# Constant full-width products among the narrow products of a router

## The chip, the cores and the metric

## What is computed

Two blocks, one after the other, on a sequence of 256 tokens of width 1024, all in fp32. The first block has two layers with attention and a grouped mixture of experts; the second has four layers with retention or attention and a plain MLP. The change concerns the mixture of experts of the first block. Cut to what matters:

```python
h = modulate(rmsnorm(x, ffn_norm_g[layer]), sh2, sc2)        # h * (1 + sc2) + sh2
x = x + g2[:, None, :] * grouped_moe(h, router_w, router_bias, w_gate, w_up, w_down)

def grouped_moe(h, router_w, router_bias, w_gate, w_up, w_down):
    scores = jax.nn.sigmoid(hf @ router_w)                    # 256 tokens x 16 experts
    # the best of 4 groups for each token, the best 2 experts in it, their shares
    for e in range(N_EXPERTS):
        a = jax.nn.silu(hf @ w_gate[e]) * (hf @ w_up[e])
        y = y + combine[:, e:e + 1] * (a @ w_down[e])
```

sh2, sc2 and g2 are rows of a product of silu(c) with a weight matrix; they are the same for all tokens.

## The kernel before

The tokens are two blocks of 128. Weights stream from HBM in pieces; ScalarE and VectorE split each into a high and a low part in fp32r, and TensorE does three fp32r products for one. Small products whose result decides the routing are in full fp32; each of them shows in the trace as two matmul instructions.

Each engine has one queue of instructions in program order. On TensorE the order is written out by hand; for each of the two mixture-of-experts layers (plan.moe0, plan.moe1), right behind the attention before it, it is:

1. `shift_product` (L1106, records on L1112): the router's weights times the shift row, eight products of 16 columns.
2. `modulations` (L1143, records on L1133): the sum over partitions of two rows of modulation, which give the scale. Eight products of one column. Together these are called the scale rows' products here.
3. `turn_x` (records on L1252): x, which the attention's output has just been added to, is transposed in sixteen blocks of 128x128 into the four banks of the PSUM tensor Y.
4. `route_product` (L1115, records on L1124): sixteen products of 16 columns, two token blocks for each of eight blocks k of the model's width. It waits for the router's weights (VectorE, L2616), and with every second k for the copy of one bank of Y (VectorE L2622 for banks 0 and 1, ScalarE L2004 for 2 and 3).
5. `keep_busy(8)` (L1231, records on L1234): eight constant products, the unit matrix times a triangle of ones, written to the first 128 columns of Y, where nobody reads them.
6. `place_tokens` (L1404 to L1408): counts of tokens for each group. It waits for VectorE, which has taken the router's sums (L2627) and made the sigmoid's and the groups' comparisons in some thirteen small steps, up to L2547.
7. `keep_busy(10)`, then the gathering of tokens and the experts' loop, for whose gate, up and down products the weights stream in.

`wait_free(pe, use)` waits until the pair of PSUM banks that `use` names has been emptied by its last reader. There are two pairs; the router's sums and the shift's stand in one and the scale rows' sums in the other.

Of the kernel before, what the change touches and what calls it, by code (L numbers as in the profile page):

```python
# [14 lines left out]
P = 128  # L15
# [362 lines left out]
def build(nc, w, table, out, rel_scratch):  # L378
# [3 lines left out]
    with ctx:  # L382
# [62 lines left out]
        ident, upto_m = squares[:, 0:P], squares[:, P:2 * P]  # L445
# [220 lines left out]
        def pair(use):  # L666
            return pairs[use.u % 2]
# [29 lines left out]
        def wait_free(eng, use):  # L697

            if use.u >= 2:
                eng.wait_ge(emptied[use.u % 2], use.u // 2)  # L700
# [280 lines left out]
        def _(pe):  # L981
# [134 lines left out]
            def route_product(m):  # L1116

                blocks = [k for bank in range(4) for k in (bank, bank + 4)]
                pe.wait_ge(router_ready, m.nth + 1)
                for i, k in enumerate(blocks):  # L1120
                    if i % 2 == 0:
                        pe.wait_ge(x_lower_copied if k < 2 else x_upper_copied, 2 * m.nth + k % 2 + 1)
                    for b in range(TB):
                        last = nc.tensor.matmul(pair(m.router)[:, b * EXPERTS:(b + 1) * EXPERTS],  # L1124
                                                turned_x[:, norm_at[k] + b * P:norm_at[k] + (b + 1) * P], router_g[:, k, :],
                                                start=(i == 0 and b == 0), stop=(i == KD - 1 and b == TB - 1))
                last.then_inc(fill_done, 1)

            def mod_product(m, out):

                wait_mod(pe, m, 8)
                for f in range(4):
                    last = nc.tensor.matmul(out[:, f:f + 1], mod_total(m)[:, f * P:(f + 1) * P], ones_col,  # L1133
                                            start=True, stop=True)
                return last
# [6 lines left out]

            def modulations(ms, use):  # L1143
                wait_free(pe, use)
                for i, m in enumerate(ms):
                    last = mod_product(m, pair(use)[:, 4 * i:4 * i + 4])
                last.then_inc(fill_done, 1)
# [83 lines left out]
            def keep_busy(n):  # L1231

                for _ in range(n):
                    nc.tensor.matmul(Y[:, 0:P], ident, upto_m, start=True, stop=True)  # L1234
# [217 lines left out]
            def experts(m):  # L1452
                turn_x(m.norm)
                route_product(m)
                keep_busy(8)
                place_tokens(m)
# [211 lines left out]
            use = plan.columns  # L1668
# [12 lines left out]
            for j in range(6):  # L1681
                token_product(plan.a_proj[j])

                use, ones_m = plan.cum[j], ones_col.to_broadcast([P, P])
                if j == 0:
# [5 lines left out]
                                     start=False, stop=True).then_inc(fill_done, 1)  # L1691
# [11 lines left out]
                if j >= 2:  # L1703
                    mod_product(STAGES["a"][j - 2], first_mods[j - 2]).then_inc(a_modulated, 1)
            attention(plan.att_a, HD, q_area, k_area, v_area, qT_area, kT_area, o_area, HD,
                      attention_done(plan.att_a), values_kept(plan.a_proj[5]), MOD[0] + G1)
            shift_product(plan.moe0)
            modulations(*plan.out_a_mods)
            experts(plan.moe0)
            for mod_use in plan.kv_mods:  # L1710
# [54 lines left out]
            use = plan.ckvT  # L1765
# [41 lines left out]
            def queries_turned(j):  # L1807
# [3 lines left out]
                      attention_done(plan.att_b), values_kept(plan.kv_up[-1]), MOD[1] + G1, queries_turned)  # L1811
            shift_product(plan.moe1)
            modulations(*plan.out_b_mods)
            experts(plan.moe1)

# [1326 lines left out]
```

## Time and profile before

| | |
|---|---|
| median of 3 runs | 2551.22 us (2542.8 to 2553.99) |
| profiled execution | 2548.41 us |
| its span, first to last instruction | 2546.6 us |
| TensorE, records of matmuls | 2426.7 us busy, 95% |
| VectorE | 1694.0 us, 67% |
| ScalarE | 1304.5 us, 51% |
| chain that ended last | TensorE 83%, VectorE 10%, ScalarE 3% |
| mean granted clock of TensorE | 0.987 |

The span is that of one execution under the profiler. "Busy" counts the time in which an engine has at least one record; a matmul's record holds its latency too, so records overlap and a busy TensorE is not one at its peak. For the time that one of a row of equal products takes, the distance between their starts, or the time in the chain, divided by their number, is to be used, not the length of a record. The chain that ended last is followed back from the last instruction, at each step to what released it.

### The profile page before, as it was taken

What the parts mean: (1) busy time and instruction counts of PE and PEld (TensorE: products, weight loads), DVE (VectorE), ACT (ScalarE), POOL (GpSimd) and SP (SyncE); (2) the same over time, 40 slices, a digit from 0 to 9 for tenths busy, and PEclk for the clock granted to TensorE, in tenths of its full rate; (3) what the DMA queues carried; (4) which work ended last, traced back from release to release, by engine and by line L of the source; (5) the groups of instructions that cost most, each with busy time, mean ns of one, the idle gap of its engine ahead of it and who ended that gap; (6) DMA issues with size and microseconds to landing.
All of it is one profiled execution on the core that took longest, in us unless ns stands there. A gap on an engine that the chain in (4) does not pass through costs nothing.

```text
span 2546.6 us, 31351 instructions
## 1 busy us (share of the span) xinstructions
PE 2426.7 (95%) x12650; PEld 2057.4 (81%) x12650; DVE 1694.0 (67%) x1521; ACT 1304.5 (51%) x1795; POOL 93.4 (4%) x121
## 2 busy tenths in 40 slices
PE   4989999999899999999999999899997999999999
PEld 3878888887788888879878888788886888987887
DVE  5767988887769787857455565565557655645654
ACT  2555777434547666634445445454455544444443
POOL 1000000111000000000000001000010000000000
PEclk8999999999999999999999999999999999999999
DMA  8815999984519897945535775155551555553553
GB/s 303 289 34 185 368 368 356 358 308 168 217 39 327 301 331 276 365 160 174 195 128 176 190 273 182 61 175 194 193 180 52 184 195 190 174 198 132 177 188 116
DMA packets 229568, 539.80 MB, mean 212 GB/s; under 512 B 20880, under 2 KB 27568, under 8 KB 229424
## 3 DMA queue, kind: packets, MB, share of 16 engines
q1 hardware_dynamic: 207264, 471.82, 53.1%
q0 software_dynamic: 15520, 59.77, 6.4%
q10 hardware_dynamic: 6640, 6.20, 1.3%
q8 instruction: 100, 1.64, 0.3%
q14 instruction: 44, 0.36, 0.0%
HBM read 533.54 MB, written 4.19 MB: 211 GB/s over the span
## 4 chain that ended last, share of the span: by engine, by line
PE 83%; DVE 10%; ACT 3%; issue 2%; DMA 1%; POOL 1%; ACTq 0%; DVEq 0%
PE pair L1041 7%; PE Y L1206 6%; PE Y L1204 6%; PE Y L1215 6%; PE pair L1469 5%; PE pair L1470 5%; PE pair L1475 5%; PE pair L1084 4%; PE pair L1077 4%; PE pair L1078 4%; PE pair L1050 4%; PE Y L1514 3%; PE Y L1516 3%; PE Y L1524 3%; PE pair L1010 2%; PE pair L1019 2%
## 5 line engine op out<-in xcount | busy, mean ns | idle before, releaser
L2316 DVE TENSOR_TENSOR w_low<-raw,w_high 128x2048 fp32r<-128x2048 f32 (+2 forms) x450 | 1016.0, 2273 | 438.8 <-ACT w_high L1858 437.4
L1858 ACT ACTIVATE w_high<-raw 128x1024 fp32r<-128x1024 f32 (+1 forms) x900 | 896.4, 1049 | 554.1 <-PE pair L1470 169.3
L1077 PE MATMUL pair<-w_high,hT 128*128 128x512 f32 (+1 forms) x596 | 233.1, 392 | 1.6 <-ACT work L1913 0.8
L1078 PE MATMUL pair<-w_high,hT 128*128 128x512 f32 (+1 forms) x596 | 231.9, 390 | 0.0
L1206 PE MATMUL Y<-w_high,gated_low 128*128 128x512 f32 x528 | 205.9, 390 | 0.0
L1204 PE MATMUL Y<-w_high,gated_high 128*128 128x512 f32 x528 | 205.9, 390 | 0.0
L1041 PE MATMUL pair<-hT,w_high 128*128 128x512 f32 x768 | 183.0, 390 | 0.5 <-DVE work L2762 0.5
L1041 PEld LDWEIGHTS pair<-hT,w_high 128*128 128x128 f32 x768 | 142.6, 188 | 29.7 <-DVE work L2762 0.9
L1469 PE MATMUL pair<-w_high,rounded 128*128 128x512 f32 x384 | 154.8, 403 | 0.8 <-DVE gated_low L2660 0.8
L1470 PE MATMUL pair<-w_high,rounded 128*128 128x512 f32 x384 | 152.2, 396 | 0.0
L1084 PE MATMUL pair<-w_low,hT 128*128 128x512 f32 (+1 forms) x596 | 146.8, 388 | 4.0 <-DVE w_low L2316 4.0
L1084 PEld LDWEIGHTS pair<-w_low,hT 128*128 128x128 f32 x596 | 110.7, 188 | 28.8 <-DVE w_low L2316 6.5
L1077 PEld LDWEIGHTS pair<-w_high,hT 128*128 128x128 f32 x596 | 113.0, 190 | 25.6 <-issue 1.6
L1078 PEld LDWEIGHTS pair<-w_high,hT 128*128 128x128 f32 x596 | 113.0, 190 | 22.5
L1215 PE MATMUL Y<-w_low,gated_high 128*128 128x512 f32 x528 | 130.4, 389 | 0.0
L1514 PE MATMUL Y<-w_high,gated_high 128*128 128x512 f32 x320 | 125.1, 391 | 3.8 <-DVE gated_low L2660 3.8
L1010 PE MATMUL pair<-hT,w_high 128*128 128x256 f32 x512 | 125.2, 285 | 0.5
L1516 PE MATMUL Y<-w_high,gated_low 128*128 128x512 f32 x320 | 124.8, 390 | 0.0
L1012 PE MATMUL pair<-hT,w_high 128*128 128x256 f32 x512 | 124.5, 283 | 0.0
L1215 PEld LDWEIGHTS Y<-w_low,gated_high 128*128 128x128 f32 x528 | 99.1, 188 | 20.6
L1206 PEld LDWEIGHTS Y<-w_high,gated_low 128*128 128x128 f32 x528 | 99.3, 188 | 19.8
L1204 PEld LDWEIGHTS Y<-w_high,gated_high 128*128 128x128 f32 x528 | 99.3, 188 | 19.8
(395 smaller groups left out, 3984.3 us busy)
## 6 DMA issues: line engine op xcount, KB each, us to landing
raw<-in_exp_w_gate SPq DMA_DIRECT2D x128, 512.0 KB, 4.6
raw<-in_exp_w_up SPq DMA_DIRECT2D x128, 512.0 KB, 4.8
raw<-in_exp_w_down SPq DMA_DIRECT2D x128, 512.0 KB, 4.6
raw<-in_w_up SPq DMA_DIRECT2D x128, 512.0 KB, 4.6
raw<-in_w_down SPq DMA_DIRECT2D x128, 512.0 KB, 4.3
raw<-in_ret_w_in SPq DMA_DIRECT2D x96, 512.0 KB, 4.7
work<-in_w_mod POOLq DMA_DIRECT2D x40, 1024.0 KB, 8.1
raw<-in_ret_w_out SPq DMA_DIRECT2D x32, 512.0 KB, 4.0
```

Of the source, the lines that this page charges most:

```text
L1041: last = nc.tensor.matmul(ps[:, f, :], high[:, k, fs], hT[:, :, kk, :], start=(kk == 0), stop=False)
L1077: nc.tensor.matmul(ps[:, b, 0:n], in_high[:, k0 + kk, bs], high[:, k, :], start=(kk == 0), stop=False)
L1078: last = nc.tensor.matmul(ps[:, b, 0:n], in_low[:, k0 + kk, bs], high[:, k, :], start=False, stop=False)
L1084: last = nc.tensor.matmul(ps[:, b, 0:n], in_high[:, k0 + kk, b * P:(b + 1) * P], low[:, k, :], start=False, stop=(kk == k_blocks - 1))
L1204: nc.tensor.matmul(y, high_in[:, kk, b * P:(b + 1) * P], high[:, k, ns], start=(first and kk == 0), stop=False)
L1206: last = nc.tensor.matmul(y, low_in[:, kk, b * P:(b + 1) * P], high[:, k, ns], start=False, stop=False)
L1215: last = nc.tensor.matmul(y, high_in[:, kk, b * P:(b + 1) * P], low[:, k, ns], start=False, stop=False)
L1469: nc.tensor.matmul(out(m, v), x_high, high[:, k, :], start=(h == 0 and k == 0), stop=False)
L1470: last = nc.tensor.matmul(out(m, v), x_low, high[:, k, :], start=False, stop=False)
L1514: nc.tensor.matmul(y, gated_high[:, v % 2, 2 * h + k, 0:WIN], high[:, k, ns], start=(first and k == 0), stop=False)
L1858: nc.scalar.activation(w_high[:, s % HIGH, part], raw[:, s % RAW, part], ACT.Copy).then_inc(high_ready, 1)
L2316: V.tensor_tensor(w_low[:, s % RAW, 0:n], part, w_high[:, s % HIGH, 0:n].bitcast(F32), ALU.subtract).then_inc(low_ready, 1)
```

## The change

Two places on TensorE get constant products of the same kind as `keep_busy` has: the unit matrix times the triangle of ones, 128 columns each, in full fp32. Three stand ahead of the scale rows' products, behind the wait for their pair of banks, and are written to the second bank of that pair. Two stand in the router's product behind its third block k and two behind its sixth, written to Y as in `keep_busy`. What is computed stays as it was.

```diff
@@ route_product
                         last = nc.tensor.matmul(pair(m.router)[:, b * EXPERTS:(b + 1) * EXPERTS],
                                                 turned_x[:, norm_at[k] + b * P:norm_at[k] + (b + 1) * P], router_g[:, k, :],
                                                 start=(i == 0 and b == 0), stop=(i == KD - 1 and b == TB - 1))
+                    if i in (2, 5):
+                        keep_busy(2)
                 last.then_inc(fill_done, 1)
@@ modulations
                 wait_free(pe, use)
+                for _ in range(3):
+                    nc.tensor.matmul(pair(use)[:, 512:512 + P], ident, upto_m, start=True, stop=True)
                 for i, m in enumerate(ms):
                     last = mod_product(m, pair(use)[:, 4 * i:4 * i + 4])
                 last.then_inc(fill_done, 1)
```

## Rows read from the trace of the kernel before

**Rows 1.** The page: span, and its part 1.

```profile
span 2546.6 us, 31351 instructions
PE 2426.7 (95%) x12650; PEld 2057.4 (81%) x12650; DVE 1694.0 (67%) x1521; ACT 1304.5 (51%) x1795; POOL 93.4 (4%) x121
```

**Rows 2.** Chain that ended last, layer 0: start us, us, what, how many.

```profile
201.75 1.69 PE pair L1112 x16
203.44 1.82 PE pair L1133 x16
205.27 3.41 PE Y L1252 x16
208.68 3.63 PE pair L1124 x32
212.31 3.36 PE Y L1234 x16
...
215.78 0.36 PE pair L1404 x2
```

**Rows 3.** The same chain in layer 1.

```profile
750.88 1.69 PE pair L1112 x16
...
754.34 3.18 PE Y L1252 x16
757.52 3.77 PE pair L1124 x32
```

**Rows 4.** Table of stretches: its us, TensorE busy (instructions), granted clock, DMA share, GB/s.

```profile
201.60:205.00 3.40, 3.40 (x33) 1.00 0.00 0
205.05:208.40 3.35, 3.35 (x18) 0.50 0.30 98
208.50:211.80 3.30, 3.30 (x33) 1.00 0.00 0
211.90:215.20 3.30, 3.30 (x17) 0.50 0.00 0
...
754.60:758.00 3.40, 3.40 (x19) 0.50 0.24 81
758.05:761.40 3.35, 3.35 (x31) 1.00 0.00 0
```

**Rows 5.** Timeline of TensorE, transposes elsewhere: start us, us, line, shape, idle before.

```profile
1526.23 0.60 PE L1252 MATMUL Y<-squares,x 128*128 128x128 f32 x4
1527.77 1.53 PE L1252 MATMUL Y<-squares,x 128*128 128x128 f32 x12 [0.94 <-DVE x L2436]
```

**Rows 6.** Timeline, weight loads of the ten constant products behind the counts, layer 0.

```profile
216.86 2.31 PEld L1234 LDWEIGHTS Y<-squares 128*128 128x128 f32 x20
```

**Rows 7.** Timeline of TensorE, runs of narrow products elsewhere.

```profile
487.78 2.73 PE L1133 MATMUL pair<-squares,work 128*128 128x1 f32 x24
525.63 1.84 PE L1133 MATMUL pair<-squares,work 128*128 128x1 f32 x16
232.51 2.29 PE L1447 MATMUL pair<-logs,rounded 128*128 128x4 f32 x20
781.50 2.29 PE L1447 MATMUL pair<-logs,rounded 128*128 128x4 f32 x20
```

**Rows 8.** Table of stretches behind those four runs, in the order of their times.

```profile
235.80:239.10 3.30, 3.30 (x10) 0.50 1.04 377
491.90:495.10 3.20, 3.20 (x9) 0.50 0.98 384
528.00:531.50 3.50, 3.50 (x17) 1.00 1.03 397
783.70:787.10 3.40, 3.40 (x16) 1.00 1.07 390
```

**Rows 9.** Timeline of VectorE in layer 0: first copy of the transposes, last step before counting.

```profile
206.76 1.29 DVE L2622 COPY work<-Y 128x512 f32<-128x512 f32 x2 [0.67 <-PE Y L1252]
...
215.47 0.17 DVE L2547 TENSOR_TENSOR route<-route 128x8 f32<-128x8 f32 x1
```

## Prediction

> **What bounds the kernel now.** I read the head of the page first: the span is 2546.6 us and TensorE has records in 95% of it [rows 1]. One number for the whole says little of two short stages, so I then read the chain of waits in the stretch where the change sits, once for each mixture-of-experts layer. In layer 0 the chain runs on TensorE alone from 201.75 to 215.67 us: the shift's sixteen narrow products, the scale rows' sixteen, the sixteen transposes of x, the router's thirty-two, then the sixteen instructions of the existing filler, and at 215.78 the counting products of the routing [rows 2]. (A product in full fp32 is two instructions, so eight shift products are sixteen rows.) The stretch from the first shift product to the end of the router's product is what the change touches. It lasts 208.68 + 3.63 - 201.75 = 10.56 us in layer 0 and 757.52 + 3.77 - 750.88 = 10.41 us in layer 1 [rows 2, 3]. Nothing idles in it: TensorE waits for nobody, so what is put there lengthens it unless it gives time back.
>
> What it could give back is the clock. The table of stretches has the granted clock beside the busy time [rows 4]. In layer 0 the engine is busy all of 201.6 to 205.0 at full clock (2.4 GHz) with narrow products, then the clock stands at 0.50 (1.2 GHz) from 205.05 to 208.40, over the transposes; it is full again while the router's product runs, and 0.50 again from 211.90 to 215.20, over the filler. Layer 1 repeats this: 0.50 from 754.60 to 758.00, full after that. So both layers show the same order: narrow products, a fall, transposes at half clock, narrow products at full clock, a second fall. I take it that a run of narrow products makes the clock fall, and that wide work brings it back. The change mixes wide work into both runs.
>
> **What the first fall costs.** The sixteen transposes take 3.41 us in layer 0 [rows 2]. At full clock four take 0.60 us and twelve 1.53 [rows 5], so one more costs (1.53 - 0.60) / 8 = 0.116 us and sixteen 1.86. The first fall costs 3.41 - 1.86 = 1.55 us a layer, and this is on the path.
>
> **What the second fall costs.** It begins at about 211.9, and the router's product ends at 212.31 [rows 2, 4]. Of the router's time only the last 0.4 us are at half clock, at most 0.2 us lost. The filler that follows takes 3.36 us slow, but its time is not on a path of its own: when the router's product ends, VectorE takes the logits and works a chain of small steps until 215.47 + 0.17 = 215.64, when the first counting product may go [rows 9]. That product comes at 215.78 [rows 2]. So a fast filler gives back at most 0.1 us; past that, VectorE is late. The price of the second fall in the kernel before is 0.2 to 0.3 us.
>
> **The change, part by part.** (a) Three full-width constant products ahead of the scale rows' products are six instructions. The twenty instructions of the same product at full clock take 2.31 us [rows 6], 0.1155 each; so 0.69 us, at half clock 16 in 3.36 us [rows 2], 0.21 each and 1.26. (b) Two products at each of two places in the router's product are eight instructions: 0.92 us fast, 1.68 slow. Both parts are on the path, since nothing idles there. They bring no wait of their own: the pair of banks has been waited for by the same function already, and the bank of Y that (b) writes has been read by then, since the router's first block waits for that copy.
> (c) The order of other engines hardly moves. With (a) VectorE gets the scale sum 0.69 us later, and so builds the router's weights later. In layer 0 it sat 0.67 us for the transposes before its first copy of them at 206.76 [rows 9]. If the transposes run fast, the copy becomes the later one: it can start about a microsecond after the scale products, takes half of 1.29 us, and the router's product could start some 1.7 us after them, against 1.86 of transposes. I take 0 for this wait and keep 0.3 as a bound.
> (d) The stage with nothing slow: shift 1.69, (a) 0.69, scale 1.82 (its last few at half clock), transposes 1.86, router 32 instructions at 0.11 us, 3.50 (sixteen shift instructions of the same form take 1.69 [rows 2], 0.106 each; 3.63 with its slow tail), and (b) 0.92. Sum 10.48 us. Against 10.56 and 10.41 that is -0.08 and +0.07, together 0.0.
> So even if the clock never falls, the filler costs what it saves: 1.61 us a layer in, 1.55 and the slow tail out. If the first fall stays in a layer, its 1.55 us come on top: +1.47 in layer 0, +1.62 in layer 1, taken as +1.5. If the second fall also comes before the longer router's product is done: in layer 0, with both falls where they were, 10.1 us have passed at 211.86 with 3.4 of them at half rate, so 8.4 us of the 10.48 are done; of the other 2.08, 1.7 are done in 3.4 slow microseconds and 0.38 fast. That is 13.9 us, +3.3 a layer, the upper bound.
>
> **Will the clock stay up?** The nearest rows are other runs of narrow products. After sixteen scale-type instructions (1.84 us) between wide products at 525.63 the clock stayed full; three such runs in the experts' loops are alike, and the first stands for them [rows 7, 8]. After twenty-four (2.73 us, 487.78) it fell to 0.50 for 491.90 to 495.10 [rows 7, 8]. After twenty router-like instructions (2.29 us) it fell in layer 0 (at 235.80) and after the same twenty in layer 1, at 781.50, it stayed full [rows 7, 8]; the outcome differs between two passes of the same code. After thirty-two in a row it fell in all three runs that rows 2 to 4 hold. The change makes 16 + 16 with 0.69 us of wide work between, and 12 + 12 + 8 with 0.46 us twice. Each run by itself is like those that kept the clock, but the wide work between two of them is short: 0.69 us, where the runs that kept it stood alone among long wide stretches. I put an even chance on the first fall in each layer, and somewhat under even on a second fall that bites.
>
> A rule of notes on the chip speaks to this. The Trainium skill, "TensorE: Matmul & The Clock Gate", section "What's actually happening", puts the half clock down to an idle engine. The trace disagrees: the fall at 205 follows 3.40 us busy of 3.40 [rows 4]. By that rule filler could change no clock here and the sum would be the cost alone, the third case below.
>
> **The rivals.**
> 1. Forecast: the first fall is avoided in one layer and stays in the other: 0.0 + 1.5 = +1.5 us. For it: the two layers meet their falls at different points of the same code (before the transposes of 205.27 in one, after those of 754.34 have begun in the other [rows 2 to 4]), so they need not fare alike.
> 2. The change does all that it says: no fall in either layer, 0.0 us. For it: the runs of sixteen. Against: 0.69 us of wide work among 4.2.
> 3. It does not do what it says, and the kernel is slower: the first fall stays in both layers, +3.0 us. The place is the shift and scale stage; the price is the filler's own 1.61 us a layer on a path without idle time; it decides as soon as one layer keeps its fall. With second falls that land in the longer router's product it goes to +6.6. Past 0.5% it would take 12.8 us, twice this bound.
> 4. The transposes do not keep the clock up by themselves, so that one fall lasts through the router's product: transposes 3.41, router 32 x 0.213 = 6.8, (b) 1.68, with 4.2 ahead 16.1 us a layer, +11 in all, 2562. Rows 4 speak against it: in layer 0 the clock was back at 208.50 behind transposes alone. The Trainium skill, same page, section "Part 4: PE-mode transpose", says that a transpose does not count as TensorE being busy; this trace disagrees, and without this sentence the case rests on rows as before.
>
> **How the numbers follow.** Case 1 has 0.42, case 2 0.20, case 3 0.35 (of it 0.15 for more than +4), case 4 0.01, and 0.02 for things not seen. The profiled execution took 2548.4 us, span 2546.6 and 1.8 around it; with +1.5 it would be 2549.9. The median of the runs is 2551.2, 2.8 above, so I predict 2551.2 + 1.5 = 2552.7. The cases alone give 2551.2 to 2557.8. The runs of before reach from 2542.8 to 2554.0, 8 us below and 3 above their median, so a median of a few runs can be off by some 5 us either way: the range is 2546 to 2559. A measurement tells about 0.5% (12.8 us) from no change. No case but the fourth comes near it, so the chance of "same" is 0.95; faster 0.02 for the runs' own spread, slower 0.03 for that and case 4.
>
> **What would show it.** In each layer of the changed kernel: six and eight more instructions of the constant product, 0.1155 us each; transposes in 1.9 us with granted clock 1.00 where the fall is gone, 3.4 where not; the stage from the first shift product to the end of the router's product at 10.4 us, or 12.0, or up to 13.9; about 3.4 us from that end to the first counting product, whatever the clock, with TensorE idle before it if the filler ran fast. The prediction is wrong if that last interval shrinks with the clock, if the clock stays low over the router's product, or if stages away from the routing differ by more than a few microseconds.

## The result and the profile after

| | before | changed |
|---|---|---|
| median, executions of the first comparison | 2549.91 us (2542.8 to 2554.1, 7) | 2564.17 us (2554.07 to 2567.37, 7) |
| ratio, 95% interval | | 1.0038 [1.002, 1.0057] |
| profiled execution | 2548.41 us | 2566.04 us |
| its span | 2546.6 us | 2564.2 us |
| mean granted clock in it | 0.987 | 0.984 |

The forecast was 2552.7 us in a range to 2559; the time is 5 us past its upper end. Two later comparisons of the same two kernels came out smaller: 2556.06 against 2553.94, ratio 0.9998 [0.9983, 1.0014], and 2557.94 against 2555.15, ratio 1.0014 [1.000, 1.0027]. The ratios are those on record for the sets of executions; the medians of the first comparison alone would give 1.0056. So the size of the loss is itself a question, and is taken up below.

The page of the changed kernel, its first lines, against [rows 1]:

```profile
span 2564.2 us, 31405 instructions
PE 2445.1 (95%) x12678; PEld 2074.4 (81%) x12678; DVE 1693.8 (66%) x1521; ACT 1304.6 (51%) x1795; POOL 93.9 (4%) x121
```

Twenty-eight more matmul instructions, as counted, and the other engines as busy as before. The span is 17.6 us longer, TensorE 18.4 us busier. Twenty-eight instructions of 0.1155 us are 3.2.

The chain that ended last, in layer 0 of the changed kernel (start us, us, what), answers to [rows 2]. L1148 are the three added products, L1135 the scale rows' (L1133 before), L1256 the transposes, L1238 the filler:

```profile
206.71 1.69 PE pair L1112 x16
208.40 0.76 PE pair L1148 x6
209.16 2.37 PE pair L1135 x16
211.53 3.52 PE Y L1256 x16
215.04 2.37 PE pair L1124 x12
217.41 1.04 PE Y L1238 x4
218.46 2.37 PE pair L1124 x12
220.83 1.04 PE Y L1238 x4
221.87 1.52 PE pair L1124 x8
```

The reader is to compare the router's instructions: 12 in 2.37 us, 0.20 each, where 32 took 3.63 before, 0.11 each. The stage, from 206.71 to 221.87 + 1.52, lasts 16.7 us; before it lasted 10.56. The table of stretches says why (us, TensorE busy, granted clock, DMA share, GB/s), against [rows 4]:

```profile
206.70:209.90 3.20, 3.20 (x32) 1.00 0.00 0
210.10:213.40 3.30, 3.30 (x17) 0.50 0.31 99
213.50:216.80 3.30, 3.30 (x18) 0.50 0.00 0
216.90:220.20 3.30, 3.30 (x17) 0.50 0.00 0
220.30:223.60 3.30, 3.30 (x17) 0.50 0.00 0
223.70:227.00 3.30, 3.30 (x17) 0.50 0.00 0
227.20:230.50 3.30, 3.30 (x29) 1.00 0.02 5
```

The clock falls once, at 210.0, in the middle of the scale rows' products, and is back only at 227.0, behind the filler that follows the router. In the kernel before it fell at 205.0, by 0.1 to 0.2 us ahead of the transposes (205.27 in the chain), and was back behind them. Layer 1 of the changed kernel, timeline of TensorE, against [rows 3]:

```profile
762.58 1.85 PE L1112 MATMUL pair<-router_w,mod 128*128 128x16 f32 x16
...
767.11 3.65 PE L1256 MATMUL Y<-squares,x 128*128 128x128 f32 x16
...
778.95 3.76 PE L1238 MATMUL Y<-squares 128*128 128x128 f32 x16
```

From 762.58 to 778.95 are 16.4 us, against 10.4. The two stages account for 6.1 + 6.0 = 12.1 of the 17.6 us. But the first shift instruction of layer 0 comes at 206.71 and not at 201.75, so 5.0 us are lost before anything changed has run. The rows for the attention ahead of it, before and then changed:

```profile
160.00:180.00 20.00, 15.27 (x122) 1.00 0.19 63
```

```profile
160.00:180.00 20.00, 15.66 (x99) 0.74 0.17 56
```

Here too the clock is down for half of the stretch in one execution and not in the other, in code that is the same. Slow stretches come and go from execution to execution, in many places of the kernel: in the first two profiles of the kernel before, one of 23.9 us at 34 us is there once and not the other time, one of 10.2 us at 165 us the other way round.

### The profile page after: what moved, and what is told of

It is laid out like the page before. It is cut to its first block, busy times and chain, and to the rows that moved or that the text cites. A ratio compares the mean times of both kernels' runs of the same rounds, so it can differ in the third digit from the quotient of the medians.

```text
span 2564.2 us, 31405 instructions
## 1 busy us (share of the span) xinstructions
PE 2445.1 (95%) x12678; PEld 2074.4 (81%) x12678; DVE 1693.8 (66%) x1521; ACT 1304.6 (51%) x1795; POOL 93.9 (4%) x121
## 4 chain that ended last, share of the span: by engine, by line
PE 82%; DVE 10%; ACT 4%; issue 2%; DMA 1%; POOL 1%; ACTq 0%; DVEq 0%; POOLq 0%
PE pair L1041 7%; PE Y L1210 6%; PE Y L1208 6%; PE Y L1219 6%; PE pair L1473 5%; PE pair L1474 5%; PE pair L1479 5%; PE pair L1084 4%; PE pair L1077 4%; PE pair L1078 4%; PE pair L1050 4%; PE Y L1518 3%; PE Y L1520 3%; PE Y L1528 3%; PE pair L1010 2%; PE pair L1019 2%
```

## Experiments

**One part at a time, and more of it.** Four kernels on one chip: the changed one again, two that leave out one hunk of the change each, and one with more of the first hunk and none of the second. The last is, against the changed kernel,

```diff
-                for _ in range(3):
+                for _ in range(8):
                     nc.tensor.matmul(pair(use)[:, 512:512 + P], ident, upto_m, start=True, stop=True)
...
-                    if i in (2, 5):
-                        keep_busy(2)
```

> The changed kernel once more, unaltered, for a second profile of its two router stages (first shift product to the end of the router's product; 16.7 and 16.3 us in the first profile, 10.56 and 10.41 before). Theory A (the half-clock stretch that starts behind the shift and scale products lasts through transposes and router's product whenever it begins before the transposes do, and the filler in the router's product is too thin at half clock to end it): each stage is either near 10.5, near 12, or at 16 to 17 us, depending on where the fall lands; the kernel 3 to 14 us slower than before. Rival B (the added products cost their own 1.6 us a layer and the rest of the first result is the luck of other stages): stages of 10.5 to 13.9 us, time +2 to +6 us.

> Only the three constant products ahead of the scale rows' products. Theory A: 0.7 us more work a layer, a fall that can still begin in the scale products; then the slow stretch may last through the router's product, without the 0.92 us (1.7 slow) of filler there: stages near 9.6, 11.2 or 15 to 16 us; time 0 to +8 us. Rival B: +1.4 us in all. Rival C (the harm is the filler in the router's product, which is absent here): stages of at most 11.3 us, time within 2 us of before.

> Only the two times two constant products in the router's product. Theory A: the first fall stays where it was in the kernel before, at the start of the transposes, and these end it: stages of 11.4 to 12.3 us where it lands so, up to 17 where it lands elsewhere; time +2 to +8 us. Rival B: +1.8 us in all. Rival C: both stages at 15 us or more, with the clock at half through the router's product.

> Eight constant products (sixteen instructions, 1.85 us) ahead of the scale rows' products and none in the router's product. Theory A: the run of narrow products is now split by a wide stretch longer than either run, so the first fall is gone in both layers: transposes in 1.9 us at full clock, stages at 1.7 + 1.85 + 1.7 + 1.86 + 3.5 = 10.6 us in every execution, time -2 to +1 us against before. Rival B: +1.85 us a layer on top of what was there, stages of 12.3 us, +3.7 us in all.

A second profile of the kernel before was taken later:

> The kernel before, unaltered, for a second profile of its two stages. Theory A: 8.8 to 15 us each, one of the values of the copies (0,0) in the sixty stages plus at most 0.3. Rival B: 10.4 to 10.6 again.

And the changed kernel and the eight products were compared once more:

> The changed kernel unaltered, for more executions: its two comparisons so far gave 1.0038 [1.002, 1.0057] and 0.9998 [0.9983, 1.0014]. Theory A: an execution's time is set by how many slow stretches it meets; the ratio comes out between the two, 1.000 to 1.003, with a spread of runs of 15 us or more. Rival D (the first comparison is the true size): 1.003 or more.

> Eight constant products ahead of the scale rows' products, none in the router's product, once more; the first comparison gave 0.9984 [0.9973, 0.9996]. Theory A: the first fall is gone in both layers again (transposes in 1.8 us), a fall may still begin in or behind the router's product; ratio 0.997 to 0.9995. Rival B: 1.001.

What they gave. The stage is read from the timeline, from the first shift instruction to the first instruction behind the router's; "fall" is the first step to 0.50 behind the first shift instruction, with how long the clock stayed there.

| kernel | ratio to before | layer 0: fall at, for; stage | layer 1 |
|---|---|---|---|
| before, first profile | | +3.4, 3.4 us; 10.56 | +3.9, 3.4 us; 10.42 |
| before, second profile | | +3.0, 20.5 us; 14.06 | +2.8, 20.5 us; 14.23 |
| changed, first profile | 1.0038 [1.002, 1.0057] | +3.4, 17.1 us; 16.68 | +3.8, 17.1 us; 16.37 |
| changed, second comparison | 0.9998 [0.9983, 1.0014] | +3.4, 17.1 us; 16.67 | +9.5, 13.7 us; 11.34 |
| changed, third comparison | 1.0014 [1.000, 1.0027] | +3.5, 17.1 us; 16.65 | +9.6, 10.2 us; 11.19 |
| three ahead of scale alone | 1.0013 [0.9993, 1.0033] | +3.8, 13.7 us; 14.67 | +9.6, 3.4 us; 9.54 |
| two times two in the router alone | 1.0016 [1.0003, 1.0029] | +3.2, 3.4 us; 12.48 | +3.1, 3.4 us; 12.55 |
| eight ahead of scale | 0.9984 [0.9973, 0.9996] | +10.7, 3.4 us; 10.66 | +9.6, 13.7 us; 11.64 |
| the same again | 0.9985 [0.9973, 0.9997] | +10.7, 3.4 us; 10.67 | +10.3, 10.2 us; 11.03 |

The row that matters most is the second. The kernel before, untouched, has the long slow stretch too. Its chain in layer 0:

```profile
206.39 1.69 PE pair L1112 x16
208.08 2.21 PE pair L1133 x16
210.29 3.52 PE Y L1252 x16
213.80 6.64 PE pair L1124 x32
220.44 3.60 PE Y L1234 x16
224.04 0.43 PE pair L1404 x2
```

Transposes in 3.52 and a router's product in 6.64 us, against 3.41 and 3.63 in [rows 2]. The 10.56 and 10.42 us that the prediction started from are not the kernel's stage but two draws of it. Rival B expected 10.4 to 10.6 again here and falls; it falls with the changed kernel's 16.7 too, which it put at no more than 13.9. Rival C, that the filler in the router's product does the harm, expected both stages with the filler in the router's product alone at 15 us or more; they were 12.5, with full clock over the first 3.0 to 3.1 of the router's 5.6 us. It expected at most 11.3 us without that filler; three ahead of scale alone has 14.67. So neither part is needed for the long stretch. Theory A comes nearest so far: 14.67 stands near its "15 to 16", 9.54 near its "9.6", 12.5 near its "11.4 to 12.3". But it missed twice. It had the clock stay down whenever the fall comes before the transposes start, and with two times two in the router alone the falls at 3.2 and 3.1 us came 0.5 and 0.7 us before they started and lasted 3.4 us only. And it had the changed kernel 3 to 14 us slower in the second comparison, where the ratio is 0.9998. For the third comparison it gave 1.000 to 1.003, which came out (1.0014); rival D, with 1.003 or more, falls.

With eight products ahead of the scale rows the first fall is gone, in four stages of four. Layer 0 of the second of these profiles:

```profile
200.07 1.85 PE L1112 MATMUL pair<-router_w,mod 128*128 128x16 f32 x16
201.77 2.03 PE L1146 MATMUL pair<-squares 128*128 128x128 f32 x16
203.63 1.84 PE L1133 MATMUL pair<-squares,gates 128*128 128x1 f32 x16
205.34 1.95 PE L1254 MATMUL Y<-squares,x 128*128 128x128 f32 x16
207.17 3.71 PE L1124 MATMUL pair<-router_g,work 128*128 128x16 f32 x32
210.73 3.66 PE L1236 MATMUL Y<-squares 128*128 128x128 f32 x16
```

10.66 us from 200.07 to 210.73, as worked out ahead (10.6). Layer 1 took 11.64 and 11.03, since there a fall came inside the router's product, which the first expectation had not. It is the only kernel of the study that is faster than before, 0.9984 and 0.9985, some 4 us, both intervals below 1; that is more than the 2 us that theory A gave it at most, and the second time inside what it expected.

**The function: sixty copies of the stage in one kernel.** Two stages an execution are too few draws. So the TensorE part of the stage was copied sixty times ahead of the real one, on constants, with its products read by nobody. A `wide` product has 128 columns, a `narrow` one 16 or 1; a copy's kind (a, r) tells how many wide products stand ahead of the scale-like ones and at each of the two places in the router-like ones. The body of a copy, without its two helpers:

```diff
+            def like_stage(a, r):
+                wide(24)
+                narrow(8, EXPERTS)
+                wide(a)
+                narrow(8, 1)
+                for _ in range(16):
+                    nc.tensor.transpose(pair(plan.moe0.router)[:, 0:P], upto_m, ident)
+                narrow(6, EXPERTS)
+                wide(r)
+                narrow(6, EXPERTS)
+                wide(r)
+                narrow(4, EXPERTS)
+                wide(8)
```

> The kernel before with sixty copies of the router stage's TensorE work put ahead of the first real one, on constants and without waits: 5.5 us of wide products, sixteen shift-like instructions, a wide products, sixteen scale-like, sixteen transposes, router-like 12 + r wide + 12 + r wide + 8, eight wide. Twelve each of (a, r) = (0,0) as before, (3,2) as changed, (3,0), (0,2), (8,0). Their products are read by nobody. Theory A (where the fall lands decides, and a slow stretch that begins before the transposes lasts through the router's product): each kind takes several discrete values; (0,0) between 8.7 and some 15 us, (3,2) between 10.4 and 17 to 18, mean of (3,2) 1.5 to 2.5 above that of (0,0); (3,0) mean within 0.5 of (0,0); (8,0) 10.5 to 11.5 nearly always. Rival B (added products cost their own time and avoid or keep a fall of 1.55 us): no kind above 14, (3,2) less (0,0) 0 to 1.6. Rival C (the filler in the router's product by itself keeps the clock down): (0,2) and (3,2) always above 15.

> As the sixty stages, but with j more wide products (0.23 us each, j from 0 to 14) ahead of each, so that the copies meet the clock's steps at all offsets; fifteen each of (a, r) = (0,0), (3,2), (0,2), (8,0). The first sixty had only part of the offsets: (0,0) had a mean of 12.36 us, (3,2) 11.32 and never a fall ahead of the transposes, though the real changed stages show 16.7. Theory A: with all offsets (3,2) shows 16 to 18 us at some, 10.3 at others, and its mean is 1 to 2.5 us above that of (0,0); (8,0) stays at 10.6 to 11.6; (0,2) is the worst, mean above 13. Rival B: (3,2) at most 13.9 at any offset. Rival E (the real stages differ from the copies by more than the clock, for instance by waits): (3,2) never above 13.9 either, while (0,0) again reaches 14.

In the first of the two the copies followed each other at nearly fixed distances, so that the clock's steps met each kind at a few places only: (3,2) had a mean of 11.32 us and (0,0) 12.36, which is the other way round from what theory A expected. (0,2) had 14.33, (8,0) 10.63, and (3,0) 10.13 where theory A had it within 0.5 of (0,0); so at those places three products ahead of scale did as well as eight. Copies of 14.6 us (0,0) and 10.1 (0,2) already speak against rivals B and C. The second kernel moved the copies (15 of each kind, and none of (3,0)). Length of a copy from its first shift-like to its first closing wide instruction:

| kind (a, r) | mean | least | most | no fall before its end | first fall over 0.3 us ahead of the transposes' place |
|---|---|---|---|---|---|
| (0,0), as before | 11.47 | 8.77 | 14.62 | 2 of 15 | 4 of 15 |
| (3,2), as changed | 12.26 | 10.33 | 16.77 | 3 of 15 | 2 of 15 |
| (0,2) | 13.95 | 10.66 | 16.35 | none | 6 of 15 |
| (8,0) | 10.64 | 10.55 | 11.49 | 12 of 15 | none |

The counts are of copies, the falls those of the trace's clock. The transposes' place is where they start at full clock: 3.5 us behind the copy's start, 4.2 with three products ahead of scale; where the clock falls sooner they start some tenths later. Two copies of the kind (3,2), the timeline of the same instructions, the first met by a fall 3.4 us behind its start, the second by none:

```profile
636.04 1.86 PE L1710 MATMUL pair<-squares 128*128 128x16 f32 x16
637.75 0.91 PE L1714 MATMUL pair<-squares 128*128 128x128 f32 x6
638.50 2.58 PE L1710 MATMUL pair<-squares 128*128 128x1 f32 x16
640.94 3.65 PE L1722 MATMUL pair<-squares 128*128 128x128 f32 x16
644.38 2.58 PE L1710 MATMUL pair<-squares 128*128 128x16 f32 x12
...
652.78 3.55 PE L1714 MATMUL pair<-squares 128*128 128x128 f32 x15
```

```profile
1207.43 1.86 PE L1710 MATMUL pair<-squares 128*128 128x16 f32 x16
1209.13 0.91 PE L1714 MATMUL pair<-squares 128*128 128x128 f32 x6
1209.88 1.84 PE L1710 MATMUL pair<-squares 128*128 128x1 f32 x16
1211.59 1.94 PE L1722 MATMUL pair<-squares 128*128 128x128 f32 x16
1213.37 1.41 PE L1710 MATMUL pair<-squares 128*128 128x16 f32 x12
...
1217.75 1.47 PE L1714 MATMUL pair<-squares 128*128 128x128 f32 x11
```

16.74 us against 10.33, on constants and without a single wait: the length is made by the clock alone, and the real stage's 16.7 is the same number. By where the first fall comes in a copy (3,2): at 3.33 and 3.37 us behind its start the clock stays down 17.1 us and the copy takes 16.7 to 16.8; at 4.06 to 4.70 us (from 0.2 us ahead of the transposes' start to 0.5 behind it) it stays down 3.4 us and the copy takes 12.4 to 13.0; at 9.0 to 9.8 us 10.8 to 11.5; three meet no fall, 10.33. For (0,0): 2.42 to 3.11 us, down 13.7 to 17.1, 14.0 to 14.6; 3.28 to 4.04, down 3.4, 10.4 to 10.7; 4.55 to 4.80, down 13.7, 12.4 to 12.6. Beside falls from 8 us on, the clock was soon back only where the fall came between 0.2 us ahead of the transposes' place and 0.6 us behind it; a fall at 3.1 us in (0,0) or 3.4 us in (3,2) is too early, one at 4.6 us in (0,0) too late. The real stages put the early edge closer: with two times two in the router alone, falls 0.28 and 0.37 us ahead of that place were soon over; with three ahead of scale alone one 0.41 us ahead of it was not. Rival B and rival E (no copy (3,2) above 13.9) fall. Over these places the change costs 12.26 - 11.47 = 0.8 us a layer, somewhat under the 1 to 2.5 that theory A gave; over the first sixty it saved 1.0. The mean depends on which places are met.

**Moving the stage.** In layer 0 the three profiles of the changed kernel have the fall at 3.42 to 3.46 us, next to where the copies (3,2) took longest; no copy of that kind has a fall between 3.4 and 4.1 us. If the stages ahead fixed that place, work put ahead of the shift's products would move it:

```diff
                 pe.wait_ge(later_loaded, 16 * N_LATER)
+                for _ in range(7):
+                    nc.tensor.matmul(pair(m.router)[:, 0:P], ident, upto_m, start=True, stop=True)
```

> The changed kernel with seven more constant products (fourteen instructions, 1.62 us) ahead of the shift's products. Layer 0's stage, counted from the first shift instruction, took 16.65 to 16.68 us in all three profiles of the changed kernel, with the fall 3.42 to 3.46 us after that instruction. Theory F (the stage's length is a function of where the clock's step meets it, and the stages ahead bring it to nearly the same place each time; the copies give the function): the step now meets the stage 1.6 us earlier in it, where the copies (3,2) take 10.3 to 11.5 us; so layer 0's stage is 10.3 to 11.5 us from the first shift instruction, no fall ahead of the transposes, and 3.6 to 4.7 us are gained with the 1.62 us of added work counted. Layer 1, whose place varies more, 10.3 to 12.9. Ratio to before 0.998 to 1.001. Rival G (the changed stage is long for itself; added work only adds): 16.7 us again in layer 0 and a time 3 us above that of the changed kernel, ratio 1.002 to 1.005.

> The kernel before with the same seven products ahead of the shift's. Its stages took 10.56 and 10.42 us in the first profile, 14.06 and 14.23 in the second. Theory F: from the first shift instruction 8.8 to 9.1 us where the fall was at 3.45 us or later, 12.4 to 12.7 where it was at 3.0; with the 1.62 us added that is 0 to 1.8 us gained a layer at most; ratio 0.9985 to 1.0005. Rival G: +1.6 us a layer on the same stages, 10.5 or 14.1 from the first shift instruction, ratio 1.001 to 1.0015.

The changed kernel with it: 2553.96 us against 2553.74, ratio 1.0003 [0.9985, 1.0021]. Its layer 0 took 16.54 us with a fall at 3.6 us, not the 10.3 to 11.5 that theory F expected; its layer 1 took 10.45:

```profile
758.78 1.86 PE L1114 MATMUL pair<-router_w,mod 128*128 128x16 f32 x16
...
762.95 1.94 PE L1258 MATMUL Y<-squares,x 128*128 128x128 f32 x16
...
769.23 2.03 PE L1240 MATMUL Y<-squares 128*128 128x128 f32 x16
```

The kernel before with it: ratio 1.0003 [0.9986, 1.002], stages of 9.13 us (fall at 8.6) and 12.59 (fall at 4.6, for 17.1 us), close to the two values that were expected. All four lengths fit the copies with falls at like places, within 0.3 us, but the first half of theory F is wrong: the place is not fixed by the code ahead. The attention ahead of it varies too: the first two profiles of the changed kernel have a slow stretch of 3.4 us from 182 us on, and this one has none there. But the third has none there either, began the stage 6 us sooner and still met the fall at 3.46 us; so why the old place came back isn't known. Rival G (the changed stage is long for itself) had 16.7 us for layer 0, and that came out; against it stand layer 1's 10.45 us, the ratio of 1.0003 where it had 1.002 to 1.005 (the interval just reaches into that), and in the kernel before 9.13 and 12.59 us where it had 10.5 or 14.1.

**A longer filler behind the router.** On top of the eight products:

```diff
-                keep_busy(8)
+                keep_busy(14)
                 place_tokens(m)
-                keep_busy(10)
+                keep_busy(15)
```

> Eight constant products ahead of the scale rows' products, none in the router's product, and the two existing fillers behind it made longer: fourteen products for eight, fifteen for ten. At full clock they take 3.2 and 3.5 us, inside the 3.6 us that VectorE needs before the first counting product and the 3.9 before the gathering. Theory A: where a second fall begins in or behind the router's product it is shorter than the 10 to 14 us seen with the short fillers, but fourteen products at half clock take 6.0 us and come 2.4 us late; the two about cancel: ratio within 0.001 of the 0.9985 of eight alone. If the second fall is what still costs: 0.997. If lateness of the filler wins: 0.9995 or more.

Ratio 1.0001 [0.9986, 1.0015]: the 4 us of the eight products are gone. The slow stretch that begins in or behind the router's product lasted 6.8 us in both layers, which is shorter than the 10.2 and 13.7 us in layer 1 with the short filler, but longer than the 3.4 in layer 0. And the filler itself ran slow for the most part and ended too late:

```profile
208.60 4.67 PE L1124 MATMUL pair<-router_g,work 128*128 128x16 f32 x32
213.11 5.68 PE L1236 MATMUL Y<-squares 128*128 128x128 f32 x28
218.63 0.28 PE L1406 MATMUL pair<-route,squares 128*128 128x4 f32 x2
```

5.5 us from the end of the router's product to the first counting product, 5.8 in layer 1, where every kernel of the table has 3.61 to 3.63 in both. That is 1.9 + 2.2 = 4.1 us more, the whole of what the eight products had gained. The expectation that the two cancel was wrong; "lateness of the filler wins" was its third case.

## Why the prediction was wrong

**Costs that held.** The added products took what was said: six instructions in 0.75 us at full clock (0.69 was said); at half clock four took 1.0 us in place of 0.84, by the distance of starts. They brought no wait. The sum with nothing slow was 10.48 us, the fastest copies (3,2) took 10.33, and layer 1 with the seven products took 10.45. The interval from the end of the router's product to the first counting product stayed at 3.6 us by the starts in the timeline (3.63 before) whatever the clock, as was said of VectorE's chain [rows 9], so long as the filler behind it was not lengthened; in layer 1 with the seven products the filler ran at full clock and TensorE then idled 1.6 us.

**The step that failed** is "I take it that a run of narrow products makes the clock fall, and that wide work brings it back". Two layers with the same order (fall, transposes, recovery) [rows 4] were read as a rule, so that a first fall was priced at the transposes alone, 1.55 us. From it came the upper bound of 13.9 us a stage. The copies show that it was back behind the transposes only if the fall came close to their start. In both layers of the profile before, the fall came within 0.4 us of their start. Three products ahead of the scale rows move the transposes 0.7 us later, and a fall 3.4 to 3.8 us behind the first shift instruction now comes 0.8 to 1.4 us ahead of them. Then the clock stays at half level over the transposes, the router's product and its filler, 17.1 us in all, and a stage takes 16.7 us, +6.1 and not at most +3.3. Four of six profiled stages of the changed kernel were of that kind. Rival 4 of the prediction described just this (16.1 us a layer, +11 in all, 2562) and had 0.01; it was set aside because the clock was back at 208.50 behind transposes alone, a row that held for one place of the fall only. The two added fillers in the router's product, which were to keep the clock up, did not raise it: in no copy and no profiled stage that has them was the clock back before the router's product ended, once it was down at one of them. In the 16.7 us stages they take turns with narrow ones, 4 wide instructions to 12, for 8.4 us at half clock. Two of the signs of being wrong that the prediction named came true: the clock low over the router's product, and 5 us of difference ahead of the routing.

**The second error** is in what it was compared with. Stages of 10.56 and 10.41 us were taken as the kernel's; a second profile showed 14.06 and 14.23. Over the moved copies (0,0) has a mean of 11.47 us. The two draws of before were from the short end, the two of the changed kernel's first profile from its long end, and their difference, 12.1 us, is not the change's mean price. The profiled real stages average 14.8 us for the changed kernel (six) and 12.3 for the kernel before (four), which would be +5 us in all; the copies say +1.6; the later two comparisons -0.5 and +3.6 (ratio less 1, times 2550), with intervals of 3 to 4 us on either side.

**The third** is the range. It ends at 2559, 1.2 us above the highest counted case (2557.8), though the same lines say that a median of a few runs can be off by 5 us either way. An execution's time moves with how much slow clock it happens to meet: over the 78 executions of six sets (the changed kernel's first comparison, and before, changed, part a, part b and eight ahead of scale in the second) the time, taken against each set's own mean as each execution's mean clock is, rises by 10.5 us for each 0.01 of mean granted clock lost, with a correlation of -0.74. The changed kernel's executions in the first comparison had a mean clock of 0.982, in the second 0.984, in the third 0.985.

**What stays open.** Two of three comparisons lie inside the forecast range (2556.1, 2557.9), the first does not, and its interval [1.002, 1.0057] does not overlap the second's. That the first met the long stretches more often fits its lower clock, but 0.0023 of clock explain about 2.4 of the 5.7 us between its mean and that of the later two together, and its stages were seen in one execution only. The kernel before was low in that comparison as well, with a mean of 2549.3 us over 7 executions where its four later sets have 2553.4 to 2555.3. The means of everything that was run, on several chips, are 2558.2 us (changed, 29) and 2553.7 (before, 101), 4.5 us apart. What else differed wasn't found. Nor was it settled what makes the place of the stage against the clock's steps; the seven products showed that it isn't the amount of work ahead alone.

**The two rules that were cited.** The rule cited from the Trainium skill, "TensorE: Matmul & The Clock Gate", "What's actually happening", that idleness brings the half clock, was again not borne out: 17.1 us at half clock with no idle time. The other, from the Trainium skill, same page, "Part 4: PE-mode transpose", that transposes don't count as busy, was set aside on one row. The runs don't bear it out either, since in a copy (3,2) a fall at 4.06 us has 0.2 us of narrow products and then only transposes behind it, and is over after 3.4 us; but its result, a clock that stays down over them, is what most stages of the changed kernel showed.

## What to carry to other kernels

Filler that is to keep TensorE's clock up has to be judged at the half clock too: placed thinly among narrow products it did not bring the clock back here, and there it cost about twice its own price (copies with a fall at 2.4 us: 16.35 us with the filler, 14.62 without, for 0.92 us of it). What did help was one piece longer than either run of narrow products that it parts (1.86 us against 1.70 and 1.71), the eight products (0.9984 and 0.9985); lengths between three and eight, and the same eight in two pieces, were not run. Don't lengthen a filler that hides in another engine's time so far that at half clock it outlasts that time: here eight products fit the 3.6 us of VectorE even at half clock, and fourteen took 5.5 to 5.8. Where a stage's length depends on where a fall of the clock meets it, one profile shows one draw: copy the stage many times at shifting distances and read the mean, before a difference of single stages is taken for the change's.

## What the hardware showed

A fall of the clock cost from nothing to 6.4 us in the same instruction sequence, by its place alone (10.33 to 16.77 us). In the kernel before as well, a slow stretch of 20.5 us began 2.8 and 3.0 us into a run of narrow products, and one of 17.1 us in the transposes behind such a run (with the seven products ahead, layer 1). A granted clock of 0.50 was there with TensorE busy 3.30 us of 3.30 in five stretches in a row of the changed kernel: being busy by the record is not what keeps it up.
